# Clipping the up sums of an expert FFN on ScalarE instead of VectorE, in a decoder block with 32 experts

## The reference, cut to what matters

```
gu = xb @ w_gate_up[e] + b_gate_up[e]
gate, up = jnp.split(gu, 2, axis=-1)
gate = jnp.minimum(gate, SWIGLU_LIMIT)
up = jnp.clip(up, -SWIGLU_LIMIT, SWIGLU_LIMIT)
act = (up + 1.0) * (gate * jax.nn.sigmoid(SWIGLU_ALPHA * gate))
y = act @ w_down[e] + b_down[e]
```

## Time and profile before

| | |
|---|---|
| median of 3 runs | 2342.4 us (2339.67 to 2343.84) |
| the profiled execution, its own time | 2346.0 us |
| its span, first to last instruction | 2344.4 us |
| mean granted TensorE clock | 0.966 of full speed |
| busy share of PE, DVE, ACT | 93%, 67%, 57% |
| units of expert weights loaded | 280 + 140 = 420, that is 35 items of 12 |

### The profile page before, as it was taken

How to read it: one execution, slowest core, us unless ns; L and a number is a source line. 1 busy time by engine, 2 the same in 40 slices (tenths; PEclk the granted TensorE clock), 3 DMA queues, 4 the chain that set the end, 5 groups by cost and what they waited for, 6 DMA issues and landing times.

```text
span 2344.4 us, 34502 instructions
## 1 busy us (share of the span) xinstructions
PE 2175.7 (93%) x10770; PEld 1797.6 (77%) x10771; DVE 1559.5 (67%) x1640; ACT 1337.9 (57%) x1523; POOL 341.2 (15%) x306
## 2 busy tenths in 40 slices
PE   7999868799499999999999999999999999999993
PEld 6889645599388878877887878778888878888873
DVE  4411256655577658677866888987666888667754
ACT  5111247733366557566746777775556777556654
POOL 1000000012302002011201122121221222122100
PEclk9999979999699999999999999999999999999997
DMA  5111200052679669689968999997776999667854
GB/s 192 55 54 54 90 1 1 25 192 100 200 233 324 218 190 379 229 287 319 379 215 288 361 359 370 362 372 251 226 239 227 322 371 358 222 222 249 302 161 161
DMA packets 265288, 536.93 MB, mean 229 GB/s; under 512 B 14478, under 2 KB 31144, under 8 KB 265132
## 3 DMA queue, kind: packets, MB, share of 16 engines
q1 hardware_dynamic: 248332, 488.26, 58.8%
q0 software_dynamic: 16896, 47.83, 8.4%
HBM read 499.29 MB, written 36.75 MB: 229 GB/s over the span
## 4 chain that ended last, share of the span: by engine, by line
PE 69%; issue 7%; DVE 6%; ACT 3%; DMA 1%; POOL 0%; DVEq 0%; ACTq 0%; SPq 0%; POOLq 0%
PE ps L686 65%; ACT hT_hi L1146 1%; PE ps L911 1%; PE ps L918 1%; DVE work L1400 1%; PE ps L832 1%; DVE hT_lo L1565 1%; DVE w_lo L1554 1%; ACT region_mem L1181 0%; DVE work L1605 0%; DVE hT_lo L1575 0%; ACT hT_lo L1194 0%; DVE weight_ring L1681 0%; DVE slots_between L1554 0%; DVE d_lam L1397 0%
## 5 line engine op out<-in xcount | busy, mean ns | idle before, releaser
L686 PE MATMUL ps<-hT_hi,hT_lo 128*128 128x512 f32 (+1 forms) x4304 | 1399.1, 389 | 12.4 <-DVE hT_lo L1575 12.4
L686 PEld LDWEIGHTS ps<-hT_hi,hT_lo 128*128 128x128 f32 x4304 | 808.5, 189 | 183.3 <-DVE w_lo L1554 18.3
L1146 ACT ACTIVATE hT_hi<-weight_ring 128x2048 fp32r<-128x2048 f32 x417 | 786.9, 1914 | 195.7 <-PE ps L686 142.0
L1554 DVE TENSOR_TENSOR slots_between<-weight_ring,hT_hi 128x2048 fp32r<-128x2048 f32 x245 | 552.7, 2285 | 140.3 <-ACT hT_hi L1146 139.7
L686 PE MATMUL ps<-slots_between,hT_lo 128*128 128x512 f32 x1344 | 527.1, 392 | 0.0
L1554 DVE TENSOR_TENSOR w_lo<-weight_ring,hT_hi 128x2048 fp32r<-128x2048 f32 x140 | 319.5, 2283 | 33.7 <-ACT hT_hi L1146 33.7
L686 PE MATMUL ps<-w_lo,hT_lo 128*128 128x512 f32 (+1 forms) x896 | 336.1, 375 | 0.0
L686 PEld LDWEIGHTS ps<-slots_between,hT_lo 128*128 128x128 f32 x1344 | 254.4, 189 | 54.2
L686 PEld LDWEIGHTS ps<-w_lo,hT_lo 128*128 128x128 f32 x896 | 168.7, 188 | 30.3
L607 POOL DMA_INDIRECT residual_rows<-work,idx_now x48 | 119.0, 2478 | 475.7 <-ACT work L1207 284.8
L601 POOL DMA_INDIRECT work<-normed_rows,idx_far x49 | 86.7, 1770 | 457.4 <-PE ps L911 293.8
(11 more groups left out here) (251 smaller groups left out, 2468.4 us busy)
## 6 DMA issues: line engine op xcount, KB each, us to landing
weight_ring<-in_w_gate_up SPq DMA_DIRECT2D x280, 1024.0 KB, 7.3
weight_ring<-in_w_down SPq DMA_DIRECT2D x140, 1024.0 KB, 5.6
weight_ring<-in_w_mix_in SPq DMA_DIRECT2D x10, 1024.0 KB, 5.9
weight_ring<-in_x SPq DMA_DIRECT2D x8, 512.0 KB, 8.0
weight_ring<-in_w_mix_out SPq DMA_DIRECT2D x4, 1024.0 KB, 5.3
work<-in_x SPq DMA_DIRECT2D x8, 512.0 KB, 4.7
residual_rows<-work SPq DMA_DIRECT2D x8, 512.0 KB, 3.3
normed_rows<-work SPq DMA_DIRECT2D x8, 512.0 KB, 3.6
```

Of the source, the lines that this page charges most:

```text
L686: return pe.matmul(o, l, r, start=first, stop=last)
L1146: act.activation(w_high_part(u), ring[:, home(u), :], ACT.Copy).then_inc(s["w_high_made"], 1)
L1554: dve.tensor_tensor(w_low_part(u), ring[:, home(u), :], w_high_part(u).bitcast(f32), ALU.subtract)\
```

## The change

ACT gets a new step `ups`, which does the clip in two passes. The first reads the up sums from PSUM (or, for a short block, the added sums in `up_b`) and writes relu(7 - x); the second works in place and writes relu(14 - that), which is clip(x, -7, 7) + 7. DVE's clip is gone, and its last step now adds 1 - 7 instead of 1 before it multiplies. `ups` stands behind the high part of unit 6 for c = 0 and behind that of unit 9 for c = 1. A third column of `limits` holds 14, and a new semaphore up_made tells DVE that the clipped sums are there; up_read is now raised by ACT.

```diff
+            def ups(it, c, kinds):
+                act.wait_ge(s["w_used"], it * 12 + (HI_SLOTS + 4 * c + 4))
+                act.wait_ge(s["a_turned"], it * 2 + (c + 1))
+                for b, kind in enumerate(kinds):
+                    rows = rows_of(kind)
+                    if kind == "short":
+                        act.wait_ge(s["sum_made"], it * 6 + (2 * c + 2))
+                    ins = act.activation(up_b[rows, b, :], up_b[rows, b, :] if kind == "short" else ps[:, out_bank("u", c, b, kinds), :],
+                                         ACT.Relu, scale=-1.0, bias=limits[rows, 0:1])
+                ins.then_inc(s["up_read"], 1)
+                act.wait_ge(s["up_read"], it * 2 + (c + 2))
+                for b, kind in enumerate(kinds):
+                    rows = rows_of(kind)
+                    ins = act.activation(up_b[rows, b, :], up_b[rows, b, :], ACT.Relu, scale=-1.0, bias=limits[rows, 2:3])
+                ins.then_inc(s["up_made"], 1)
...
                 up_rest(it, 0, kinds)
+                ups(it, 0, kinds)
                 high_unit(it, 7)
...
                 up_rest(it, 1, kinds)
+                ups(it, 1, kinds)
                 with act.If(size_next > 0):
...
-                dve.wait_ge(s["w_used"], it * 12 + (HI_SLOTS + 4 * c + 4))
-                dve.wait_ge(s["a_turned"], it * 2 + (c + 1))
                 if "short" in kinds:
+                    dve.wait_ge(s["a_turned"], it * 2 + (c + 1))
                     b = kinds.index("short")
                     add_rest(it, 2 * c + 2, up_b[0:SHORT, b, :], out_bank("u", c, b, kinds))
-                for b, kind in enumerate(kinds):
-                    place = up_b[rows_of(kind), b, :]
-                    if kind == "short":
-                        dve.wait_ge(s["sum_made"], it * 6 + (2 * c + 2))
-                    ins = dve.tensor_scalar(place, ps[:, out_bank("u", c, b, kinds), :] if kind == "full" else place, LIMIT, -LIMIT,
-                                            ALU.min, ALU.max)
-                ins.then_inc(s["up_read"], 1)
-                dve.wait_ge(s["up_read"], it * 2 + (c + 2))
+                dve.wait_ge(s["up_made"], it * 2 + (c + 1))
                 dve.wait_ge(s["silu_made"], it * 2 + (c + 2))
                 for b, kind in enumerate(kinds):
                     rows = rows_of(kind)
-                    ins = dve.scalar_tensor_tensor(out=up_b[rows, b, :], in0=up_b[rows, b, :], scalar=1.0, in1=sig_b[rows, b, :],
+                    ins = dve.scalar_tensor_tensor(out=up_b[rows, b, :], in0=up_b[rows, b, :], scalar=1.0 - LIMIT, in1=sig_b[rows, b, :],
```

More of the change, by code:

```diff
@@ L230, in hymba_kernel @@
         eps = sb("eps", [P, 1])
-        limits = sb("limits", [P, 2])
+        limits = sb("limits", [P, 3])
         ssq = sb("ssq", [P, 10])
@@ L293, in hymba_kernel @@
             "bias_in", "bias_high", "bias_low", "picked",
-            "w_high_made", "w_low_made", "limits_made", "below_made", "rest_made", "sum_made", "w_used", "up_read", "sig_made", "silu_made", "a_made",
+            "w_high_made", "w_low_made", "limits_made", "below_made", "rest_made", "sum_made", "w_used", "up_read", "up_made", "sig_made", "silu_made", "a_made",
             "a_turned", "a_high", "a_low", "y_made", "pe_item", "act_item", "dve_item",
@@ L574, in _ @@
             pool.nop().then_inc(s["consts_made"], 1)
-            for n, value in enumerate((LIMIT, ALPHA * LIMIT)):
+            for n, value in enumerate((LIMIT, ALPHA * LIMIT, 2.0 * LIMIT)):
                 pool.memset(limits[:, n:n + 1], value).then_inc(s["limits_made"], 1)
@@ L1139, in _ @@
             act.preload_act_table(ACT.Sigmoid)
-            act.wait_ge(s["limits_made"], 2)
+            act.wait_ge(s["limits_made"], 3)
             def high_unit(it, u):
```

## The result

The changed kernel takes 2359.05 us (median of 6 runs, 2354.78 to 2362.91), against 2343.12 us of the kernel before (6 runs). The ratio is 1.0065, with a 95% interval of 1.0045 to 1.0086, that is 10.5 to 20.2 us slower, 15.9 by the medians. The forecast was 11.3 us slower and 2353.7 us, with a range of 2347 to 2360. Its profiled execution took 2360.76 us, with a span of 2359.1.

A forecast was written before the change was run, and what follows sets the result against it. PE was taken to set the time, following DVE from unit 9's low part on in single items. Single items 6.6 us plus full+short items 4.7 gave 11.3 us (9.1 to 14.2) on 2342.4, so 2353.7 us, range 2347 to 2360.

The forecast's parts named there:

- What bounds the kernel: Expert items: PE sets the time, and in single items follows DVE by 0.05 us from unit 9's low part on.
- Single items: 22 single items, unit 7 to DVE's last step: the step starts 0.30 us later (0.22 to 0.38), 6.6 us in all.
- Full+short items: Nine items: last step 1.19 to 1.35 us later against 0.71 us cover at unit 9; 0.52 us each, 4.7 us.
- What would show it: Signs in the new profile, among them PE's a_low(1) wait growing from 0.83 to about 1.1 us, single items taking 37.5 us.
- What costs nothing: Full+full items (2.6 us cover), the c = 0 passes, and a_high(1) behind the new passes (1.1 us left): no loss.
- The rule weighed against it: Skill's claim that back-to-back ACTIVATEs overlap by about 93 ns; would give about 7.6 us; rejected for dependent passes 0.03 us apart.
- only the single items pay: Rival, 14%: the full+short items' term vanishes, leaving +4.8 us (2347.2 us) or +6.6 us (2349.0 us).
- DVE's relief reaches PE: Rival, 4%: without its clip DVE is 0.64 us ahead, shrinking PE's 15 waits at unit 10; 9.6 us less, 2332.8 us.
- No change: Rival, 8%: both terms at the low end or below, or partly swallowed by PE's ten unexplained stops; under 4.7 us.
- ACT becomes the bound: Rival, 4%: ACT gets 136 us more work and its c = 1 pairs reach PE whole, 68 us, 2410 us.

The follow-up runs named there:

- repeated run: The changed kernel measured once more, unaltered, beside the kernel before: 2363.5 us against 2345.78, ratio 1.0061 (1.0043 to 1.008).
- run with one value for both waits: Changed kernel with up_made counted from one, so DVE's two waits ahead of its last step have equal values: 2358.76 us against 2345.78 of the kernel before.
- c = 0 alone: Changed kernel with ACT clipping for c = 0 only, DVE clipping as before for c = 1: 2342.53 us against 2344.49 of the kernel before.
- three passes: Changed kernel with a third in-place ACT pass that changes no value: 2392.39 us, ratio 1.0209 to the kernel before.
- run without the clip: Kernel before with DVE's clip left out and nothing added on ACT: 2332.42 us against 2342.2, ratio 0.9953.
- reordered kernel: Kernel before with a_low(1) and the low part of unit 11 ahead of x_low where a single item is next: 2328.55 us against 2343.72.

## Why the prediction was right

**What bounds the kernel**: right. PE follows DVE from the low part of unit 9 on in single items; the distance is again 0.05 us, and it now holds in the full+short items too.

**Single items**: the mechanism was right and the size too small, 0.30 us for some 0.34 (0.33 in the mean of the eleven items, 0.36 in the repeated run). Of the steps in the sum, unit 7 to ACT (0.03 forecast, 0.04 measured), the two passes (0.69 and 0.72 both) and the gap between them (0.03, 0.04) were right. The handover to DVE was set at 0.03, with up to 0.08 more as a bound, and took 0.12, just beyond the bound. The run with one value for both waits shows that 0.09 of it came from a wait that stood on a sequencer's step; the prediction had seen that row, but priced it as a bound for both handovers, and the first of them took none of it. The 0.30 was the middle of two bounds (0.22 and 0.38) and not a sum, so that it came close is in part luck. And the row was reckoned in an item where DVE had been 1.28 us behind unit 7, while in every other one it was 1.25: with 1.60 after the change, the shift at unit 9 alternates between 0.33 and 0.35 us.

**Full+short items**: 0.52 us forecast, 0.59 measured at unit 9 and 0.59 to 0.69 over a whole item, 5.8 us for the nine. The step starts 1.30 us later instead of 1.19 to 1.35, against a cover of 0.71; it is the same handover. Together the items account for 22 x 0.34 + 5.8 = 13.3 us, where 11.3 were forecast. The 15.9 by the medians lie above that, but the interval from 10.5 holds it, and so does that of the repeated run. What the rest of 2.6 us is, if it is anything, stays open.

**What would show it**: one line was wrong. PE's wait at unit 10 was to grow from 0.83 to about 1.1 us. It stayed at 0.84, and the shift came as a new wait of 0.24 us at unit 9. Unit 9 ends as much later as a_low(1) does, so the wait between them cannot grow. The sum was not touched by that, since it counted DVE's shift and not the wait.

**What costs nothing**: right. c = 0 alone cost nothing, and full+full items did not wait. a_high(1) kept 1.3 us of room, and ACT did not become the bound: with 4.1 us more of work in a single item (three passes, 32.38 against 28.32) the loss was still that of the chain alone.

**The rule weighed against it**: the row was the right choice. The dependent passes stood 0.03 to 0.04 us apart, and only the pair on two blocks overlapped (1.34 us).

**Rivals**: "only the single items pay" is refuted by the run in which only they used ACT, +7.9 us. "DVE's relief reaches PE" named a true lever, as the run without the clip shows, but its condition, that the sums are there within 0.6 us of unit 7, was not met. "No change" and "ACT becomes the bound" are refuted by the 10.5 to 20.2 us of the result.

## What to carry to other kernels

An engine with time to spare is no free place for a step. What counts is whether the step lies on the row from the bound engine's last result back to its next start: two passes of 0.7 us and two handovers replaced DVE's own clip there and cost some 0.34 us an item, while the same two passes elsewhere in the item cost nothing. Before moving work, look at what stands ahead of the late step in its own engine's queue. Here moving two instructions of x_low out of its way, with no work saved, brought 15 us by the medians. When a wait is taken away in such a queue, look for the next one: it came back at once at unit 11.

## What the runs showed of the hardware

- A DVE instruction started 0.03 us after the ACT instruction that released it where the wait for ACT stood on the instruction itself. Where it stood on a step of DVE's sequencer just ahead, it started 0.12 us after it (a register step of 0.04 us) or 0.11 (a semaphore step of 0.02 us), in 70 places each.
- Two ACTIVATEs of which the second waits for the first stood 0.03 to 0.04 us apart; a pair on two different blocks took 1.34 us, 0.1 less than twice 0.72.
- PE's stops that the profile gives no reason for are not the same in all executions. One between two single items was 4.97 us in the kernel before and 4.80 in the changed one, but 0.47 us at the same place in the reordered kernel:

```profile
1058.71 0.79 PE L686 MATMUL ps<-mem_there,picked 128*128 128x512 f32 x1 [4.97 <-issue]
```

```profile
1055.77 0.49 PE L686 MATMUL ps<-mem_there,picked 128*128 128x512 f32 x1 [0.47 <-issue]
```

  The time passes in a branch of PE's sequencer into the body of the next item (L372, the kernel before and then the reordered one, ns):

```profile
L372 PEldq COMPARE_BRANCH  x1: 4422/4422/4422, 1053.8 to 1053.8; - x1
```

```profile
L372 PEldq COMPARE_BRANCH  x1: 208/208/208, 1055.1 to 1055.1; - x1
```

  What that branch waits for is not shown. The stop costs more than its own length. Just behind it the granted clock is 0.50, that is 1.2 instead of 2.4 GHz:

```profile
1056.00:1062.00 6.00, 3.29 (x8) 2.62 (x9) 2.97 (x2) 1.91 (x1) 2.17 (x1) 0.50 1.02 276
```

  The item with it takes 44.37 us in the kernel before. The same item takes 38.01 us in the kernel with c = 0 alone on ACT, whose trace has 0.62 us there, so the stop is worth about 6.3 us, more than a third of the change looked for. Eight of the 14 traces have it. That is why the times of single items are given here beside every median. The second reordered kernel shows how the two go together. Of its 15 items eleven gain 0.79 to 0.89 us and three, at a turn of the loop, 1.21 to 1.26; the fifteenth is the one with the stop. With some 1.2 us for it too the items make about 14 of the 15.2 us by the medians.
